# Seven block products in place of eight for half of each feed-forward part's down outputs

## The reference

```python
def conv_ffn(h, w_up, conv_w, conv_b, w_down):            # blocks 1 and 2: parts f0 and f1
    T = h.shape[1]
    a, b = jnp.split(h @ w_up, 2, axis=-1)
    a_pad = jnp.pad(a, ((0, 0), (CONV_WIDTH - 1, 0), (0, 0)))
    a = sum(a_pad[:, j:j + T] * conv_w[j] for j in range(CONV_WIDTH)) + conv_b
    return (jax.nn.silu(a) * b) @ w_down
...
    ffn = (jax.nn.silu(n2 @ w_gate) * (n2 @ w_up)) @ w_down   # block 3: part f2, no convolution
```

## Time and profile before

| | us |
|---|---|
| median of 3 runs | 893.28 |
| lowest and highest | 893.13, 893.43 |
| profiled execution | 893.27 |
| its span (first to last instruction) | 891.5 |
| busy: TensorE | 884.7 (99%) |
| VectorE | 648.3 (73%) |
| ScalarE | 495.6 (56%) |
| GpSimd | 43.8 (5%) |

### The profile page before, as it was taken

How to read it: one execution, slowest core, us unless ns; L and a number is a source line. 1 busy time by engine, 2 the same in 40 slices (tenths; PEclk the granted TensorE clock), 3 DMA queues, 4 the chain that set the end, 5 groups by cost and what they waited for, 6 DMA issues and landing times.

```text
span 891.5 us, 18689 instructions
## 1 busy us (share of the span) xinstructions
PE 884.7 (99%) x7879; PEld 860.4 (97%) x7879; DVE 648.3 (73%) x1189; ACT 495.6 (56%) x851; POOL 43.8 (5%) x54
## 2 busy tenths in 40 slices
PE   8999999999999999999999999999999999999998
PEld 7999999999999998889999999999988999999998
DVE  6997557887767689785887767678688586565664
ACT  6763566555545567575565546547447464454451
POOL 1000001000000001000000000001142000000000
PEclk9999999999999999999999999999999999999999
DMA  8753344565464544633546554553162265556541
GB/s 325 287 190 124 124 177 135 199 243 190 166 217 186 197 150 170 236 113 101 214 182 237 211 200 170 214 212 131 60 237 96 95 230 198 197 180 218 200 151 48
DMA packets 26003, 160.68 MB, mean 180 GB/s; under 512 B 3009, under 2 KB 4929, under 8 KB 7361
## 3 DMA queue, kind: packets, MB, share of 16 engines
q1 hardware_dynamic: 25344, 158.45, 49.1%
q10 hardware_dynamic: 576, 1.05, 0.4%
HBM read 158.18 MB, written 1.05 MB: 179 GB/s over the span
## 4 chain that ended last, share of the span: by engine, by line
PE 97%; DVE 1%; DMA 1%; issue 0%; SPq 0%; ACT 0%
PE ps L417 96%; PE ps L433 2%; DMA raw<-in_w 1%; DVE arena L1769 1%; DVE wl L1317 0%; DVE arena L1753 0%; DVE arena L1825 0%; DVE wl L1533 0%; SPq L2629 0%; DVE arena L1844 0%; DVE xt L1513 0%; DVE arena L1766 0%; ACT wh L2261 0%; DVE arena L1748 0%; DVE arena L1762 0%
## 5 line engine op out<-in xcount | busy, mean ns | idle before, releaser
L1317 DVE TENSOR_TENSOR wl<-raw,wh 128x1024 fp32r<-128x1024 f32 x280 | 329.6, 1224 | 121.5 <-ACT wh L2113 121.2
L417 PE MATMUL ps<-xh,wh 128*128 128x256 f32 (+1 forms) x1260 | 350.1, 278 | 1.5 <-DVE wl L1533 1.1
L417 PE MATMUL ps<-xl,wh 128*128 128x256 f32 (+1 forms) x1260 | 348.5, 277 | 0.0
L417 PE MATMUL ps<-xh,wl 128*128 128x256 f32 (+1 forms) x1260 | 348.3, 277 | 0.0
L2113 ACT CAST wh<-raw 128x1024 fp32r<-128x1024 f32 x280 | 277.3, 1048 | 115.0 <-PE ps L417 105.1
L417 PEld LDWEIGHTS ps<-xh,wh 128*128 128x128 f32 x1260 | 236.5, 188 | 3.1 <-DVE wl L1533 1.3
L417 PEld LDWEIGHTS ps<-xl,wh 128*128 128x128 f32 x1260 | 236.5, 188 | 0.0
L417 PEld LDWEIGHTS ps<-xh,wl 128*128 128x128 f32 x1260 | 236.5, 188 | 0.0
L417 PE MATMUL ps<-fh,wh 128*128 128x256 f32 x528 | 145.7, 276 | 0.0
L417 PE MATMUL ps<-fl,wh 128*128 128x256 f32 x528 | 145.7, 276 | 0.0
L417 PE MATMUL ps<-fh,wl 128*128 128x256 f32 x528 | 145.7, 276 | 0.0
(11 more groups left out here) (263 smaller groups left out, 1058.7 us busy)
## 6 DMA issues: line engine op xcount, KB each, us to landing
raw<-in_w SPq DMA_DIRECT2D x144, 1024.0 KB, 4.9
raw<-in_w SPq DMA_DIRECT2D x8, 256.0 KB, 7.1
xt<-in_x ACTq DMA_DIRECT2D x4, 256.0 KB, 5.4
arena<-in_mem SPq DMA_DIRECT2D x1, 1024.0 KB, 8.4
out<-xt SPq DMA_DIRECT2D x8, 128.0 KB, 1.9
arena<-in_sel SPq DMA_DIRECT2D x3, 256.0 KB, 6.0
small<-in_small SPq DMA_DIRECT2D x1, 623.0 KB, 6.7
memkv<-in_gmask SPq DMA_DIRECT2D x1, 512.0 KB, 11.3
```

The costliest lines, as they stand in the source:

```text
L417: return pe.matmul(out, lhsT, rhs, start=start, stop=stop, skip_group_check=True)
L1317: v.tensor_tensor(L[:, s], src[:, s], f32(H[:, s]), ALU.subtract).then_inc(*w_lo.up(split(i, a)))
```

## The change

For the pairs p = 0 to 9 of each part, output columns 512 to 1023 are made another way. The pair's tokens (2 halves of 128) x inner features (2 chunks) and its weights (2 chunks x 2 halves of 256 output columns) are seen as 2x2 blocks, and their product is made from seven block products in Winograd's form of Strassen's scheme, in place of eight. Tokens are now stationary (128x128) and weights move (256 columns), so these results have tokens on partitions. The seven products gather over the ten pairs in four banks `q0` to `q3` (one in each half bank, the last half free). Each takes three matmuls, so a pair has 24 + 21 in place of 48.

What this takes besides:
- GpSimd (`quarter_sums`): per pair four sums of weight blocks (128x256 each) from `raw` into `t7`, and after the gated products four sums of token blocks (128x128 each) into `s7`.
- ScalarE: a down unit is cast as a half of 1024 columns, the three plain blocks (768) into `coh`, and the sums `t7` (1024) into the unit's second half; `sums_high` casts `s7` (512), at the end of each loop, ahead of the casts of the next down unit. `sums_high(p)` waits for GpSimd, and for TensorE's use of the sums before.
- VectorE: low parts of the same sizes, `sums_low` between the down unit's and the next up unit's.
- The next load into a down unit's slot of `raw` waits for the low part of the weight sums, which stands last, and for that of the plain blocks.
- Up units from u4 on take turns in two banks in place of four, since q2 and q3 have the others. `variance` of the meta tokens is made one loop earlier in f1.
- At the end, in d10, after its first four output blocks (24 matmuls) TensorE waits until VectorE has combined the seven products (`quarters`: seven operations of 128x256 behind a copy by ScalarE), turns them with eight transposes back to features on partitions, and makes d10's other four blocks in two banks of their own; VectorE adds both results to x. `quarters` stands on VectorE ahead of the adds for acc4 and acc5 and of the next unit's low part that was first after the loop.

The diff, cut to its core:

```diff
 KOUT = [4, 5, 6, 7, 0, 1, 2, 3]
...
 WOFF = {U[n]: 32 for n in ("m0v0", "m0v1", "m1v0", "m1v1", "Av0", "Av1", "kvv", "Cv0", "Cv1")}
...
+    b7h, b7l = (lambda k: coh_[:, 560 + k % 2 * 768:1328 + k % 2 * 768]), (lambda k: col_[:, 560 + k % 2 * 768:1328 + k % 2 * 768])
+    s7h, s7l = coh_[:, 0:512], col_[:, 0:512]
+    s7, t7 = arena[:, 9152:9664], arena[:, 9664:10688]
+    u7 = [arena[:, 4016 + n * 256:4272 + n * 256] for n in range(4)]
+    def t_slot(buf, i):
+        a = S[i] % NH * HS + HW + 32
+        return buf[:, a:a + HW]
...
+        def seven(tag, p):
+            i, k, f = U[f"{tag}d{p}"], SEVENTH[U[f"{tag}d{p}"]], 2 * p
+            B = [(b7h(k)[:, n * 256:(n + 1) * 256], b7l(k)[:, n * 256:(n + 1) * 256]) for n in range(3)]
+            W = [(t_slot(wh, i)[:, n * 256:(n + 1) * 256], t_slot(wl, i)[:, n * 256:(n + 1) * 256]) for n in range(4)]
+            sums_ = [(s7h[:, n * 128:(n + 1) * 128], s7l[:, n * 128:(n + 1) * 128]) for n in range(4)]
+            part = lambda g, x: (fch(fh_, g)[:, x:x + 128], fch(fl_, g)[:, x:x + 128])
+            t.wait_ge(*f_bl.at(k))
+            t.wait_ge(*f_sl.at(k))
+            t.wait_ge(*w_low(i, 1))
+            for n, (A, M) in enumerate(((part(f, 0), B[0]), (part(f + 1, 0), B[1]), (sums_[1], W[1]), (sums_[2], W[2]),
+                                        (sums_[0], W[0]), (sums_[3], B[2]), (part(f + 1, 128), W[3]))):
+                name = f"{tag}q{n // 2}"
+                if p == 0 and n % 2 == 0:
+                    t.wait_ge(*ps.vacant(name))
+                O = ps[name][:, n % 2 * 256:n % 2 * 256 + 256]
+                mm(O, A[0], M[0], p == 0 and n % 2 == 0, False)
+                before = mm(O, A[1], M[0], False, False)
+                last = mm(O, A[0], M[1], False, p == 9)
+                if p == 9 and (n % 2 == 1 or n == 6):
+                    last.then_inc(*ps.full(name))
+            if p in range(1, 9):
+                last.then_inc(*f_su.up(SEVEN[tag] // 10 * 8 + p - 1))
+            return before, last
...
+        def quarters_turned(tag):
+            for n in range(2):
+                name = f"{tag}ct{n}"
+                P = ps.open(name, ps.place[f"{tag}q{n}"][0])
+                t.wait_ge(*ps.vacant(name))
+                t.wait_ge(*f_c.at(SEVEN[tag] // 10 * 3 + 2))
+                for k in range(4):
+                    t.wait_ge(*ps.done(f"{tag}q{k}"))
+                for k in range(2):
+                    for r in range(2):
+                        a = r * 512 + (2 * n + k) * 128
+                        last = tr(P[:, k * 256 + r * 128:k * 256 + (r + 1) * 128], t7[:, a:a + 128])
+                last.then_inc(*ps.full(name))
...
             if p == 0:
-                for b in range(4, 8):
+                if not wide:
+                    for n, b in enumerate([6, 7] + rest_of[tag]):
+                        ps.open(f"{tag}q{n}", b)
             if p < 10:
+                H, L = (v3(wslot(buf, i)[:, 0:2048 if wide else 1024], 1024 if wide else 512) for buf in (wh, wl))
+                for j in range(2):
+                    t.wait_ge(*f_l.at(22 * m + 2 * p + j))
+                if not wide and p:
+                    seven(tag, p)
                 for j in range(2):
...
-                    for o in range(8):
-                        acc = banks[4 + o // 2][:, (o % 2) * 256:(o % 2) * 256 + 256]
+                    t.wait_ge(*w_low(i, j if wide else 0))
+                    for o in range(8 if wide else 4):
+                        acc = ps[f"{tag}acc{4 + o // 2}"][:, (o % 2) * 256:(o % 2) * 256 + 256]
                         cs = slice(o * 128, (o + 1) * 128)
                         last = mm3(acc, H[:, j, cs], L[:, j, cs], fch(fh_, f), fch(fl_, f), f == 0 and o % 2 == 0, False)
-                    last.then_inc(*f_used.up(20 * m + f))
+                    if wide or p:
+                        last.then_inc(*f_used.up(20 * m + f))
+                if not wide and p == 0:
+                    for f, last in enumerate(seven(tag, 0)):
+                        last.then_inc(*f_used.up(20 * m + f))
                 used[i] = f_used.at(20 * m + 2 * p + 1)
                 return
...
             for o in range(8):
-                acc = banks[4 + o // 2][:, (o % 2) * 256:(o % 2) * 256 + 256]
+                name = f"{tag}acc{4 + o // 2}"
+                if o == 4 and not wide:
+                    quarters_turned(tag)
+                if o in (4, 6) and not wide:
+                    ps.open(name, bank_a())
+                    t.wait_ge(*ps.vacant(name))
+                acc = ps[name][:, (o % 2) * 256:(o % 2) * 256 + 256]
...
+            if tag in SEVEN:
+                rest_of[tag] = was[2:4]
+                turns["a"][:] = was[0:2]
...
+                if i in SEVENTH:
+                    k = SEVENTH[i]
+                    d.wait_ge(*w_hi.at(split(i, 0)))
+                    v.tensor_tensor(L[:, 0:HW], src[:, 0:HW], f32(H[:, 0:HW]), ALU.subtract).then_inc(*w_lo.up(split(i, 0)))
+                    d.wait_ge(*f_bh.at(k))
+                    v.tensor_tensor(b7l(k), src[:, HW + 256:UW], f32(b7h(k)), ALU.subtract).then_inc(*f_bl.up(k))
+                    d.wait_ge(*w_hi.at(split(i, 1)))
+                    v.tensor_tensor(t_slot(wl, i), t7, f32(t_slot(wh, i)), ALU.subtract).then_inc(*w_lo.up(split(i, 1)))
+                    continue
...
+            def sums_low(p):
+                k = SEVEN[tag] + p
+                d.wait_ge(*f_sh.at(k))
+                v.tensor_tensor(s7l, s7, f32(s7h), ALU.subtract).then_inc(*f_sl.up(k))
+            def quarters():
+                k = SEVEN[tag] // 10 * 3
+                q0, q1, q2, q3 = (f"{tag}q{n}" for n in range(4))
+                lo, hi = slice(0, 256), slice(256, 512)
+                c1, u2, u3, u4 = u7
+                d.wait_ge(*f_c1.at(SEVEN[tag] // 10))
+                d.wait_ge(*ps.ready(q1))
+                v.tensor_tensor(u2, ps[q1][:, lo], c1, ALU.add).then_inc(*f_c.up(k))
+                v.tensor_tensor(t7[:, 0:256], ps[q0][:, hi], c1, ALU.add).then_inc(*ps.freed(q0))
+                d.wait_ge(*f_c.at(k))
+                d.wait_ge(*ps.ready(q2))
+                v.tensor_tensor(u3, ps[q1][:, hi], u2, ALU.add).then_inc(*ps.freed(q1))
+                v.tensor_tensor(u4, ps[q2][:, lo], u2, ALU.add).then_inc(*f_c.up(k + 1))
+                d.wait_ge(*ps.done(q1))
+                d.wait_ge(*ps.ready(q3))
+                v.tensor_tensor(t7[:, 512:768], u3, ps[q3][:, lo], ALU.subtract).then_inc(*ps.freed(q3))
+                d.wait_ge(*f_c.at(k + 1))
+                v.tensor_tensor(t7[:, 256:512], ps[q2][:, hi], u4, ALU.add).then_inc(*f_c.up(k + 2))
+                v.tensor_tensor(t7[:, 768:1024], ps[q2][:, lo], u3, ALU.add).then_inc(*ps.freed(q2))
+            def quarters_in():
+                for n in range(2):
+                    d.wait_ge(*ps.ready(f"{tag}ct{n}"))
+                    x2 = xt_[:, (4 + 2 * n) * T:(6 + 2 * n) * T]
+                    v.tensor_tensor(x2, ps[f"{tag}ct{n}"][:, :], x2, ALU.add).then_inc(*ps.freed(f"{tag}ct{n}"))
...
             for p in range(11):
                 if p:
                     rests(f"{tag}u{2 * p}", 2)
+                    if tag in SEVEN:
+                        sums_low(p - 1)
                     rests(f"{tag}u{2 * p + 1}", 2)
...
+            if tag in SEVEN:
+                quarters()
             after = NAMES[U[f"{tag}d10"] + 2:][:1]
             rest(*after, halves=(0,))
             for q in range(4):
                 name = f"{tag}acc{4 + q}"
+                if q == 2 and tag in SEVEN:
+                    quarters_in()
+                if q >= 2 and tag in SEVEN:
+                    d.wait_ge(*ps.done(f"{tag}ct{q - 2}"))
                 d.wait_ge(*ps.ready(name))
...
+                if i in SEVENTH:
+                    k = SEVENTH[i]
+                    a.wait_ge(*d_w[i % NR].at(i // NR))
+                    a.wait_ge(*used[SPLIT[S[i] - NH]])
+                    s.copy(H[:, 0:HW], src[:, 0:HW]).then_inc(*w_hi.up(split(i, 0)))
+                    if k % 10 >= 2:
+                        a.wait_ge(*used[U[NAMES[i][:3] + str(k % 10 - 2)]])
+                    s.copy(b7h(k), src[:, HW + 256:UW]).then_inc(*f_bh.up(k))
+                    a.wait_ge(*f_ta.at(4 * k + 3))
+                    s.copy(t_slot(wh, i), t7).then_inc(*w_hi.up(split(i, 1)))
+                    continue
...
+            def sums_high(p):
+                k = SEVEN[tag] + p
+                a.wait_ge(*f_sa.at(4 * k + 3))
+                if p:
+                    a.wait_ge(*(f_su.at(SEVEN[tag] // 10 * 8 + p - 2) if p > 1 else used[U[f"{tag}d0"]]))
+                s.copy(s7h, s7).then_inc(*f_sh.up(k))
...
                 if p:
                     casts(f"{tag}d{p - 1}", 2)
+                if tag in SEVEN and p < 10:
+                    sums_high(p)
...
+            if tag in SEVEN:
+                a.wait_ge(*ps.ready(f"{tag}q0"))
```

(37 more changed lines are left out.)

27 lines of the change are left out of this document (21 added, 6 removed).

## The result

The changed kernel takes **937.5 us** (median of 4 runs, 931.7 to 939.5); the kernel before, in runs between them on the same chip, 893.4 us. The ratio is 1.048, 95% interval 1.046 to 1.051: slower by 44 us. The forecast was 936, with a range of 897 to 957. Two of the experiments have one execution each in a slower state (1795.9 us in E10, 927.3 us in E11), and their medians and ratios leave it out.

What follows compares the result with a forecast made beforehand. TensorE bound the kernel before; the changed one was to be bound in f0 and f1 by VectorE's loop with ScalarE and GpSimd: 893.3 + 20.7 + 20.7 + 1.5 = 936 us, range 897 to 957.

Steps and rivals of the forecast that it cites:

- TensorE's busy share: Sign over the whole kernel that the forecast is right: TensorE's busy share falls under 96%, from 99% before.
- its waits inside the loops: Sign in f0 and f1: TensorE idle 1.5 to 2 us a pair, waiting for low parts of VectorE.
- What TensorE gains and pays: TensorE, all parts: 90 fewer matmuls at 0.1133 us save 10.2 us, transposes add 3.3; 886.4 us if nothing waited.
- No rival: Rivals for the whole kernel: port held whole (945 to 970) 0.15, port gives way (896 to 905) 0.18, not slower 0.07.
- The loop, 17.9 us: f0 and f1: VectorE, ScalarE and GpSimd's loop takes 17.9 us where TensorE needs 15.98, adding 10.8 us a part.
- a sign of a longer loop: f0 and f1: if GpSimd's 128x128 operations cost nearly as much as its 128x256 ones, the loop exceeds the forecast.
- The hold on VectorE, 0.49 and 0.24 us: Beside VectorE: each GpSimd operation holds it about 0.49 us for 128x256, 0.24 for 128x128; bounds 0.2 and 0.64.
- The start, u5 4.2 us late: Start of f0 and f1: token sums ahead of d0's casts and the weight sums' holds make u5 start 4.2 us late.
- d10, 16.9 us late: Before the end of f0: start and loop delays, less 1.0 us of earlier slack, make d10 start 16.9 us late.
- The end, 3.8 us: In d10 of f0 and f1: 2.7 us waiting for the quarters' combination and 1.1 us of transposes.
- f0 and f1 +20.7 each: Total extra cost of f0, with start, loops and end together: 20.7 us, and f1 as much.
- f2 +1.5: f2: VectorE's loop about 16.6 us, start absorbed by slack; only transposes and their latency are left, +1.5 us.

Runs made afterwards that it cites:

- E10: Change in f2 alone, ScalarE's down-unit casts ahead of the token sums' cast in every pair, one matmul split 240+16 behind each seven products: 893.1 us, ratio 0.9997 to before.
- E11: Change in all parts, down-unit casts ahead of the token sums' cast in every pair, a matmul split 240+16 behind every seven products: 907.9 us.
- E5: Changed kernel with ScalarE's cast of the token sums moved behind the casts of the next down unit: 920.6 us.
- E2: Changed kernel with each of GpSimd's eight sums cut to 16 columns, all waits kept, output not the reference's: 912.8 us.
- E3: Changed kernel with GpSimd's full-size sums on fixed data into scratch, ScalarE casting fixed data without waiting for them, output not the reference's: 916.7 us.
- E4: As E2, but the 21 matmuls of the seven products load weights and move 256 tokens, output not the reference's: 898.3 us.
- E9: Kernel before the change, with 21 of each pair's 144 matmuls loading tokens and moving weights, output not the reference's: 902.6 us.
- E7: As E5, with one matmul a pair behind the seven products issued as 240 and 16 columns: 917.9 us.
- E8: As E5, with the seven products as 42 matmuls that load weights and move 128 tokens, without the eight transposes: 967.0 us.

## Why the prediction was right, and where it was not

The mechanism that carried the sum, VectorE, ScalarE and GpSimd in one loop that binds f0 and f1, is shown: by the changed trace, by E5 (one hand-over out of it, 16.9 us) and by E2 and E3. The total came within 2 us, but by its parts less well: f0 and f1 were forecast 4.6 us too high, f2 and the stage ahead of it 6.9 too low. So near a hit was luck in part: loops forecast some 7 us too long in f0 and f1 together (141.4 us against 8 x 17.29 = 138.3 and 8 x 17.16 = 137.3) made up for half clock and slow pitch, which were not in the sum. Two of the forecast's own signs did not come: TensorE's busy share is 97% (904.3 of 936.9) and not under 96%, and its waits inside the loops are 0.7 to 1.3 us and not 1.5 to 2, because at the slow pitch its own loop is 16.5 to 16.6 us and not 15.98.

- **"What TensorE gains and pays", -10.2 us: the step that failed.** The pitch of 0.1133 us was carried over to a kernel in which other operands are loaded. Measured 117.7 ns; by E2 against E4 it costs 14.5 us, more than the whole gain. No rival had it. In the changed kernel it shows less in f0 and f1, whose loops of 17.2 to 17.3 us are longer than TensorE's 16.5 in any case.
- **The loop, 17.9 us**: 17.29 and 17.16 in the mean of eight. The single stations were right to some tenths: cast of the token sums forecast 4.45 us behind the gated product, found 4.65 (249.96 to 254.61); L1399 6.05, found 6.26. The end came sooner (17.54 in place of 17.9), though GpSimd's last token sum took as long as its last weight sum in the mean (978 and 988 ns), which the forecast had named as a sign of a longer loop.
- **The hold on VectorE, 0.49 and 0.24 us**: the two low parts from 251.38 took 2.88 us in place of the 2.36 of the earlier trace rows, beside two token sums: 0.26 each. Beside the weight sums two gated products took 1.85 us (265.65) in place of the 0.83 of the earlier trace rows, about 0.5 for each. Right. GpSimd's own 0.38 us for 128x128 was too low: 0.46 alone. By the Trainium skill, SBUF — State Buffer, section "SBUF: two separate sides", the whole instruction would be lost (0.46 us alone); here GpSimd's operation was stretched to 1.3 to 1.4 us and VectorE lost a quarter of a microsecond, so the trace agrees that they delay each other and not with the length.
- **The start, u5 4.2 us late**: 4.19 in f0, 4.02 in f1. Right. E11 shows part of the cause: with d0's casts ahead of the token sums the waits are 2.21 and 2.50. **d10, 16.9 us late**: 14.4 in f0 (336.32 against the 321.90 of the earlier trace rows); the loops were shorter.
- **The end, 3.8 us**: 2.30 of waiting (forecast 2.7) and the transposes. Right, but for the clock: from d10's start to the part's end f0 lost 5.2 us (19.6 less 14.4).
- **Not in the sum: half clock behind long waits**, some 8 us in the changed kernel. The profile of before could not show it, for there TensorE's only two waits of over 0.6 us lie in the first 10 us; that half clock can be added to a stall I had not reckoned with.
- **f0 and f1 +20.7 each**: 19.6 and 17.2. **f2 +1.5**: 4.3, and mostly by another cause than mine: not VectorE's loop of 16.6, but TensorE's pitch. From f2's first down matmul to the end of the span E4 takes 153.7 us, E2 157.9 and the changed kernel 159.9: 4.2 for the pitch, 2.0 for GpSimd's work. With it, the 4.1 us between f1 and f2, of which TensorE waits 2.46 for the last adds to x (the forecast had "no more there") and about 1.7 are half clock behind that wait.

Three steps on the chip, taken in this order, make up the difference: GpSimd's work and hand-overs 24.8 (changed kernel less E2), pitch 14.5 (E2 less E4), and 4.9 that remains in E4: the 10.2 us saved, with 3.3 of transposes and some 12 at starts and ends against them. Of these 12 (a remainder, not measured) E4's trace shows 8.1 as waits ahead of u5, in d10 and behind f1, and 1.7 as half clock. 24.8 + 14.5 + 4.9 = 44.2.

Open: what in TensorE makes the two pitches, and what exactly switches them. E4 and E9 show that the swapped operands are needed and enough; whether the number of matmuls in the group (21, an odd one) has a part, or the waits and increments at the same place, was not tried apart. Nor is it known why some waits are followed by half clock and others of the same length are not. And how much of the 24.8 would remain if GpSimd's operations had their undisturbed length in the same chain was not tried.

## What to carry to other kernels

When a change removes instructions from the engine that is the bound, look first whether the pitch of those that stay holds: compare busy time with the count, and a busy time that rises while the count falls is the sign. Look at the granted clock with it, for half clock raises busy time as well (some 8 of the 19.6 us here). In an in-order queue, an instruction that waits for a slow helper engine belongs behind everything that the bound waits for: one cast's place was worth 17 us. And a long stall of TensorE can cost more than its length, for the clock may be low behind it.

## What the hardware showed that I had not expected

- Two pitches of the same 128x256 matmul at full clock without a gap, 113.3 and 117.7 ns, each kept for a hundred matmuls and more. A group of 21 that loads tokens and moves weights can switch from one to the other (E9: every loop). Behind the waits of 4.19 and 4.02 us in the changed kernel u5 ended at 113, behind those of 1.39 and 1.70 in E2 it stayed at 118. A split matmul in each loop kept 113 where u5 had it (f0 and f1 of E7; without it E5 went back to 118) and not where u5 went at 118 (f2 of E7); with u5 split too, f2 had 113 (E10).
- A matmul of 128 moving columns with a new weight block takes 111 ns, nearly as much as one of 256 at 113 (E8).
- The granted clock went to 1.2 GHz at the end of TensorE's waits of 2.30, 2.46, 4.02 and 4.19 us in the changed kernel and stayed there for 3.4 or 6.8 us; behind the 2.21 and 2.50 us ahead of u5 in E11, and behind the wait of 2.30 in f1's d10 in the changed kernel, it did not. The wait of 2.47 us at the end of f1 was followed by 3.4 us at 1.2 GHz in E11 and by none in E5, so its length alone does not decide.
- A GpSimd operation can take three times as long beside one of VectorE: the fourth token sum took 1.32 us beside a low part, and 0.46 where VectorE stood still, at f0's start in E7:

```profile
171.35 0.46 POOL L2769 TENSOR_TENSOR arena<-arena 128x128 f32<-128x128 f32 x1
```
